# Later places for the fourth head's ninth outer products, norm and store, and for the products of pooled tiles, in a one-core transformer step

## Time and profile before

| | |
|---|---|
| median of 3 runs | 2721.09 us (2719.21 to 2724.32) |
| span of the profiled execution | 2720.1 us, clock 0.991 |
| PE, DVE, ACT, POOL busy | 97%, 52%, 33%, 24% |
| stage around the change | about 576 to 754 us of the span |

### The profile page before, as it was taken

The page is one execution under the profiler, slowest core; times in us unless marked ns, Lnnn a source line. Parts: engine busy times, 40 slices in busy tenths (PEclk is TensorE's granted clock), DMA queues, the critical chain, the costliest instruction groups (busy, mean ns, idle before and its releaser), DMA issues.

```text
span 2720.1 us, 37395 instructions
## 1 busy us (share of the span) xinstructions
PE 2643.3 (97%) x16040; PEld 2354.7 (87%) x16040; DVE 1424.9 (52%) x1680; ACT 898.4 (33%) x940; POOL 652.8 (24%) x218
## 2 busy tenths in 40 slices
PE   5999999998999999999999999999999999999997
PEld 3787877797988879999999999999999888888875
DVE  5323232346576457655555545555566354444578
ACT  4333333332311154333333333333333333333343
POOL 0000000000000001344443444344434333333440
PEclk9999999999999989999999999999999999999998
DMA  9775757422463142332233323332334645464566
GB/s 378 281 277 209 272 207 255 153 90 91 176 218 118 64 159 80 108 108 88 93 108 108 96 86 106 108 103 84 101 108 158 239 174 213 174 213 166 208 231 233
DMA packets 179384, 438.11 MB, mean 161 GB/s; under 512 B 9980, under 2 KB 25732, under 8 KB 173076
## 3 DMA queue, kind: packets, MB, share of 16 engines
q1 hardware_dynamic: 176916, 430.48, 45.4%
q10 hardware_dynamic: 2304, 5.24, 0.5%
HBM read 401.83 MB, written 33.85 MB: 160 GB/s over the span
## 4 chain that ended last, share of the span: by engine, by line
PE 62%; DVE 11%; DMA 10%; POOL 10%; issue 4%; ACT 3%; SPq 0%; POOLq 0%; ACTq 0%; DVEq 0%
PE ps L2355 6%; PE ps L2356 6%; PE ps L2357 6%; DMA raw_w<-w_gu_b 5%; PE ps L2278 5%; PE ps L2280 5%; PE ps L2279 5%; PE ps L2031 5%; PE ps L2033 5%; PE ps L2032 5%; POOL raw_w L945 3%; PE ps L2011 3%; DVE w_lo L1666 3%; POOL low L942 2%; POOL raw_w L948 2%
## 5 line engine op out<-in xcount | busy, mean ns | idle before, releaser
L1666 DVE TENSOR_TENSOR w_lo<-raw_w,w_hi 128x1024 fp32r<-128x1024 f32 x264 | 336.6, 1276 | 297.6 <-ACT w_hi L1210 294.7
L1210 ACT ACTIVATE w_hi<-raw_w 128x1024 fp32r<-128x1024 f32 x264 | 270.1, 1054 | 601.0 <-POOL raw_w L951 368.9
L2278 PE MATMUL ps<-x_hi,w_hi 128*128 128x320 f32 x1408 | 435.7, 309 | 1.0 <-DVE w_lo L1666 0.7
L2279 PE MATMUL ps<-x_lo,w_hi 128*128 128x320 f32 x1408 | 435.1, 309 | 0.0
L2280 PE MATMUL ps<-x_hi,w_lo 128*128 128x320 f32 x1408 | 435.1, 309 | 0.0
L942 POOL TENSOR_TENSOR low<-raw_w 128x1024 f32<-128x1024 f32 x41 | 103.7, 2528 | 1098.8 <-DMA raw_w<-w_gu_b 1058.7
L1801 DVE TENSOR_TENSOR x_lo<-low,x_hi 128x2560 fp32r<-128x2560 f32 (+2 forms) x55 | 221.3, 4027 | 262.6 <-ACT x_hi L1303 262.6
L2355 PE MATMUL ps<-w_hi,x_hi 128*128 128x512 f32 x880 | 343.8, 391 | 7.7 <-DVE w_lo L1932 2.8
L2356 PE MATMUL ps<-w_lo,x_hi 128*128 128x512 f32 x880 | 343.1, 390 | 0.0
L2357 PE MATMUL ps<-w_hi,x_lo 128*128 128x512 f32 x880 | 342.9, 390 | 0.0
L2278 PE MATMUL ps<-low_r,w_hi 128*128 128x320 f32 x1072 | 333.0, 311 | 1.5 <-DVE w_lo L1666 1.5
(11 more groups left out here) (238 smaller groups left out, 4362.9 us busy)
## 6 DMA issues: line engine op xcount, KB each, us to landing
raw_w<-w_gu_b SPq DMA_DIRECT2D x180, 512.0 KB, 5.6
low<-w_ada SPq DMA_DIRECT2D x68, 1024.0 KB, 6.9
raw_w<-w_down SPq DMA_DIRECT2D x55, 1024.0 KB, 5.2
low<-hidden_scratch SPq DMA_DIRECT2D x33, 1280.0 KB, 6.0
raw_w<-w_in_b SPq DMA_DIRECT2D x33, 1024.0 KB, 9.1
x_raw<-w_ada SPq DMA_DIRECT2D x25, 1024.0 KB, 15.2
raw_w<-w_out SPq DMA_DIRECT2D x16, 1024.0 KB, 5.1
hidden_scratch<-high SPq DMA_DIRECT2D x44, 320.0 KB, 5.9
```

What stands on the lines that cost most here:

```text
L1210: nc.scalar.activation(weight(0, w), src, ACT.Copy).then_inc(prod_hi, 1)
L1666: nc.vector.tensor_tensor(weight(1, n), src, weight(0, n).bitcast(F32), ALU.subtract).then_inc(prod_split, 1)
L2278: mm(out, wh, version(v, 0, k), start=first and k == 0, stop=False)
L2279: mm(out, wh, version(v, 1, k), start=False, stop=False)
```

## The change

For the last head alone, `outer9` moves one quarter later in both directions (for the backward one that is behind the evacuation of unit 26), `rms` one quarter, `norm` and `o_store` two quarters. `poolmm` of groups 0 to 2 moves two quarters later and now comes before `pool` of the next group in the list; `poolmm 3` keeps its quarter but is now before `x_norm 4`. `pool` with j = 0 of groups 1 to 3 moves one quarter later. `pool 0 0` keeps its place and is now ahead of `outer9 3 0`. `norm 3` and `poolmm 1` stay neighbours, now behind quarter 1 of unit 28. No other item moves.

```diff
     for h in range(HEADS):
 
         after_k = 4 * (where["k", h, 0] + 1)
+        last = h == HEADS - 1
+        ninth = 1 if last else 0
+        rms, norm, store = (27, 29, 31) if last else (26, 27, 29)
         for at, item in (
...
-                         (10, ("vT", h, 1)), (10, SLOT), (12, ("outer", h, 0)), (12, INNER), (12, ("outer9", h, 0)),
+                         (10, ("vT", h, 1)), (10, SLOT), (12, ("outer", h, 0)), (12, INNER),
+                         (12 + ninth, ("outer9", h, 0)),
...
-                         (22, ("outer", h, 1)), (22, INNER), (22, ("outer9", h, 1)),
+                         (22, ("outer", h, 1)), (22, INNER), (22 + ninth, ("outer9", h, 1)),
...
-                         (26, ("rms", h, 0)), (27, ("norm", h, 0)), (29, ("o_store", h, 0))):
+                         (rms, ("rms", h, 0)), (norm, ("norm", h, 0)), (store, ("o_store", h, 0))):
             put(0, after_k + at, item)
+    for g in range(4):
+        put(where["p", g, 1], 9 if g < 3 else 7, ("poolmm", g, 0))
     for j in range(8):
-        put(where["p", j // 2, j % 2], 4, ("pool", j // 2, j % 2))
+        put(where["p", j // 2, j % 2], 5 if j and j % 2 == 0 else 4, ("pool", j // 2, j % 2))
...
-    for g in range(4):
-        put(where["p", g, 1], 7, ("poolmm", g, 0))
```

## The result

The changed kernel is slower by 0.12%: the ratio to the kernel before is 1.0012, 95% interval 1.0007 to 1.0018, with medians of 2723.08 us (20 runs) and 2718.56 us (20 runs); by the ratio that is 3.3 us, by the medians 4.5. Beside the last experiments it was timed once more: 1.0014, interval 1.0006 to 1.0023. The forecast was 2719.9 us, 1.2 us less than before; it has the sign wrong, though the time lies in the range and inside the 0.2% taken as no change. That the time itself is only 3.2 us off is in part luck: it was worked out from the median of three runs, 2721.09 us, and that of the 20 is 2.5 us lower.

A forecast was written before the change was run, and what follows sets the result against it. TensorE, busy 97% of the span, was taken as the bound, with at most 11.7 us to win. Order effects of -3.4 us plus 2.2 for the clock gave -1.2 us: 2719.9 us, range 2715.5 to 2724.5.

The forecast's parts named there:

- Ninth forward, pool (0,0) ahead of it: Forward ninth outer product: its 1.45 us wait goes, mix waits 2.4 us behind DVE's pooled tile; D = +0.95.
- Products of group 0 moved away: Unit 26, second half: PE waits 5.0 us for unit 25's evacuation, behind cum on ACT, replacing 2.44; D = +3.5.
- Pool (1,0), ninth backward: Backward ninth outer product: PE waits 0.4 us for DVE in place of 1.62; D = +2.3.
- Norm and group 1: Norm transposes wait 0.5 us in place of 3.19; second pooled group at full clock saves 3.0; D = -3.4.
- Rival (d): ACT's way to the scaling is 2.8 us longer, 1.4 us behind each of two table loads: 2722.7 us, chance 0.03.
- The clock: Behind the new 5.0 us wait in unit 26 the clock falls, costing 2.2 us; bounds 0 to 5.8.
- The step that took 43% of all cold time: Cold matmuls start every 0.26 us against 0.15, so low clock of 3.4 or 6.7 us costs 1.5 or 2.9.
- The statement that 2.44 us do no harm: The old 2.44 us wait at 613 left the clock up: the pooled products behind it ran in 4.35 us.
- The rest: Later pooled groups: no wait at group 2's products, 0.2 us at group 3's, then the old sequence shifted by D.
- Rival (b): Clock falls twice, at the new wait and the norm transposes, so 3.0 us are not saved: 2722.9 us, chance 0.15.

The follow-up runs named there:

- products0_back: Changed kernel with the products of group 0 and pool (1,0) back at their old places; ratio to the kernel before 0.9991.
- cum_late: Changed kernel with cum of head 3, backward, one quarter later, behind the evacuation of unit 25 on ACT; ratio to the kernel before 1.0011.
- pool01_alone: Changed kernel with only pool (0,1) moved on DVE, behind the evacuation of unit 24 and ahead of the gates; ratio to the kernel before 1.0006.
- norm_only: Kernel before with only rms, norm, o_store of head 3 and the products of group 1 (pool (2,0) behind them) moved as in the change; ratio 0.9985.
- group2_early: Changed kernel with groups 2 and 3 as before: group 2's products behind unit 29, pool (3,0) behind quarter 30q0; ratio to the kernel before 0.9999.

## Why the prediction was wrong

By its own steps, D again being PE's delay against before, with the 2.74 us from ahead of the stage taken off.

- *Ninth forward, pool (0,0) ahead of it:* right. Wait 2.25 for 2.4, D = 595.10 - 591.35 - 2.74 = +1.0 for +0.95. What it lacked is the clock, whose cost at this wait the sum put at nothing: it fell there in six of the eight profiles that have the wait, and where mix was wholly at low clock that cost 1.7 us (4.03 for 2.34).
- *Products of group 0 moved away:* right in size, 4.83 for 5.0, and products0_back shows that they were the cover. The reason given, cum ahead of the evacuation on ACT, is what ended the wait, but it was incomplete: cum_late shows that the pooled tile holds the evacuation directly too, and pool01_alone that with the tile gone cum still holds it for 3.17 us.
- *Pool (1,0), ninth backward:* right, 0.37 for 0.4.
- *Norm and group 1:* right. 0.25 for 0.5, products at full clock. ACT's chain from the evacuation to the Exp took 5.8 us (666.91 to 672.68) for the forecast's 5.7 (662.6 to 668.3), with the Ln at 670.86, 0.02 us behind its table load (669.56 + 1.28). Rival (d) is out. The drain of about 1.38 us that the Trainium skill states (ScalarE: Activation LUTs, "What ACT_TABLE_LOAD costs") does not show in this trace either.
- *The clock:* it fell where forecast. In the first profile that cost, from the release at 623.30 to the next quarter at 628.31, 5.0 us for 3.3 at full clock, some 1.7 us, for 2.2. The step that took 43% of all cold time overlooked that cold time inside a wait costs nothing: of the 6.8 us, which alone would give 2.9, some 3 were such. The statement that 2.44 us do no harm holds in four profiles of five (norm_only).
- *"The rest":* **this step failed.** "No wait" before and in the groups 2 and 3 was argued from the products and the slack of pool (3,1) alone. The evacuation's own wait for the pooled tile, a line printed with the kernel's other waits, was left out. The waits measured 0.93 and 1.74 us. In D they are 1.2 and 2.0, since the matmuls do not overlap across a wait, and 0.6 more came before the products of group 3, since the late evacuation holds back the split and with it pool (3,1): 3.8 us together. D goes from -2.0 behind the products of group 1 to -0.8 at those of group 2 (710.26 - 701.25 - 7.05 - 2.74), and at the products of group 3, where -1.2 was forecast, it is 738.64 - 734.10 - 2.74 = +1.8. group2_early takes the 1.74 and 0.6 us away again, and norm_only has the 0.93 with group 1 moved alone.

-1.2 + 3.8 is +2.6; the first profile has +1.8, since the clock cost 0.5 us less and the steps ahead came out 0.3 us better, the second +3.8, since the clock fell at mix too. The +3.3 of the ratio (1.0012) lies between; with six falls in eight an estimate from the two profiles is 0.25 x 1.8 + 0.75 x 3.8 = +3.3. So two terms of the sum failed, the waits left out of "the rest" (3.8 us) and the clock at mix (about 1.5, three quarters of the 2.0 us between the two profiles). Rival (b) came nearest in time, 2722.9, by a mechanism that did not happen: the clock never fell at the transposes in the changed kernel. Two falls, yes, but the other one at mix.

What stays open: in what share of the executions the clock falls at mix, and what decides it. Profiles give six of eight, of which the changed kernel's own are one of two; the timed runs do not tell it apart.

## What to carry to other kernels

When a step is moved later, ask of each thing that it hands on, and of each that waits for what it hands on, how much slack it had; here the products were harmless, and the pooled tile behind them, and the evacuation behind that, had 5.4 and 4.2 us for a move of 7.05. List every wait of an instruction before naming one as its reason: an evacuation with two reasons does not come free when one is taken away. And before moving a reader later, look whether the work it waits for can go earlier, into idle time or ahead of work that nobody waits for (pool (0,1) ahead of the gates).

## What the runs showed of the hardware

The clock fell at waits as short as 2.25 us, and not always: at 1.45 and 1.62 us in none of three profiles each, at 2.25 before the 64-row matmuls of mix in six of eight, at 2.44 before full 512-column products in one of five, at 3.17, at 3.19 with transposes and 1.03 us more, at 3.5 with 1.6 us shortly ahead of it, and at 4.83 us in all (one, three, two and four profiles). It did so inside the wait or up to 2 us behind it: 1.8 us into the 4.83 us in the first profile of the changed kernel, 1.6 us behind the 3.52 us in that of cum_late. What cold time costs depends on what falls into it: 1.7 us of the 6.8 in the one, 3.0 of the 6.8 in the kernel before. The time at low clock in the stage ran from 0 to 10.4 us over the fourteen profiles. So one and the same kernel differs by 2 us in this stage from one execution to the next (224.2 and 226.1), and a wait of 2 us or more can cost another 1.7, or 3.0 as at the norm transposes before.
